# Inverting the delta-rule triangles by diagonal blocks of 32

## The chip, the cores and the metric

The kernel runs on one core of one Trainium2 chip. The metric is the device time of one execution in microseconds (us); the time of a kernel is the median of its runs. The five engines are TensorE (PE), VectorE (DVE), ScalarE (ACT), GpSimd (POOL) and SyncE (SP), and each works through its own queue of instructions in order, held back by semaphores.

## The reference, cut to what matters

A two-layer network on 256 tokens of width 1024 runs: a first block (feed-forward, a mixer, cross attention to a memory, feed-forward) twice, then a second block twice. The mixer has a part with eight heads of 64 that keeps a state and updates it token by token:

```
def step(state, inp):
    r_t, w_t, k_t, v_t, kk_t, a_t = inp
    sa = jnp.einsum('bhij,bhj->bhi', state, -kk_t)
    state = (state * w_t[:, :, None, :] + sa[..., None] * (kk_t * a_t)[:, :, None, :]
             + v_t[..., None] * k_t[:, :, None, :])
    return state, jnp.einsum('bhij,bhj->bhi', state, r_t)
```

The kernel does not run this loop. It cuts the 256 tokens into four chunks of 64. Within a chunk the tokens' corrections depend on each other through a strictly triangular 64 by 64 matrix N per head, and solving for them needs the inverse of I − N. There are 8 heads and 4 chunks, so 32 such inverses in each of the two layers. Everything is float32.

## The kernel before, in words

The 256 tokens lie on 128 partitions in two tiles, t = 0 and 1. A tile holds two chunks: c = 0 on partitions 0 to 63 and c = 1 on 64 to 127. The eight heads are split in two groups g of four (even and odd heads). So there are four groups (t, g), the list `GROUPS4`, each with 4 heads x 2 chunks = 8 triangles, and one PSUM bank for each (4 + 2t + g).

The masked triangles N lie in `MK` (slot 0 of its third dimension), written by DVE at L1137. `T2` holds for each group two running matrices of 4 x 64 columns: the inverse transposed (slot 0) and the inverse (slot 1). `XG` holds an intermediate product.

The inverse is built by doubling. `pe_rw_inv0` (L1161) computes the untransposed triangle; `dve_rw_inv0` masks both down to pairs of tokens and adds the identity (L1170, L1172, L1176). Then five levels, 1 to 5, each join two inverted blocks of size b = 2, 4, 8, 16, 32 to one of 2b: PE computes N times the inverse into PSUM (L1185), DVE masks it to the blocks below the diagonal (L1205), PE multiplies that with the inverse from the other side, once for the inverse transposed (L1194) and, except in level 5, once for the inverse (L1197), and DVE adds the result to both (L1210). Each product is one 64*64 matmul for each head and chunk, the two chunks one after the other on two diagonal quarters of the PE array. Within a level all four groups do their first products, then all four their second ones.

The order of the work is written out by hand, one list for each engine: `pe_mix`, `act_mix`, `dve_mix`. Between the levels stand other steps: on PE transposes for the memory's keys (`pe_kv_turn`, L1660), transposes to token order (L1098), units of the weight stream (L343 to L345), the bonus (L1331) and gate products (L1343, L1344); on DVE the low parts of those transposes (L459), two scalings (L1085, L1088) and the split of weights into a high and a low part (L325), for which ACT makes the high part (L316) and SP loads the raw weights into a ring of four. After level 5 the chunks are solved in turn: `pe_rw_rhs` (L1236), `pe_rw_u` (L1270, which reads `T2`), `pe_rw_state`. `pe_rw_rhs` waits for the last additions of level 5.

Of the kernel before, what the change touches and what calls it, by code (L numbers as in the profile page):

```python
# [9 lines left out]
ACT = mybir.ActivationFunctionType  # L10
ALU = mybir.AluOpType
AX = mybir.AxisListType.X

P = 128
S = 256
NT = S // P
# [6 lines left out]
HD = 64  # L23
# [30 lines left out]
def constants():  # L54

    s = np.arange(P)[:, None]
    t = np.arange(P)[None, :]
    same = (s // 64) == (t // 64)
    c = {}
    c["ident"] = (s == t)  # L60
    decay = -float(np.exp(-0.5))
    c["cums"] = np.concatenate([decay * ((s <= t) & same), decay * ((s < t) & same)], 1)
    c["ones64"] = np.concatenate([(s // 64 == 0), (s // 64 == 1)], 1)
    c["cum"] = np.concatenate([(s + P * k) <= np.arange(S)[None, :] for k in range(NT)], 1)

    i, j = s % 64, np.arange(64)[None, :]
    c["ident64"] = i == j
    c["mask4"] = np.concatenate([i < j, i <= j, i < j, i <= j], 1)
    for lv in range(6):
        b = 1 << lv  # L70
        c[f"low{lv}"] = ((i // (2 * b)) == (j // (2 * b))) & ((i // b) % 2 == 1) & ((j // b) % 2 == 0)
    c["lowT0"] = ((i // 2) == (j // 2)) & (i % 2 == 0) & (j % 2 == 1)
# [57 lines left out]
class Program:  # L130
# [60 lines left out]
    def places1(self):  # L191
# [3 lines left out]
        xn = self.XN.rearrange("p a b -> p (a b)")  # L195
# [9 lines left out]
        self.ZR = self.E2  # L205
        self.MK = self.mem(NT, 8, 4, HD)
        t2 = self.mem(2048)
        self.T2 = [[t2[:, 512 * (2 * t + g):512 * (2 * t + g + 1)].rearrange("p (a h c) -> p a h c", a=2, h=4)
                    for g in range(2)] for t in range(NT)]
        self.XG = [[xn[:, 1024 + 256 * (2 * t + g):1280 + 256 * (2 * t + g)].rearrange("p (h c) -> p h c", h=4)  # L210
                    for g in range(2)] for t in range(NT)]

        flat = lambda x: x.rearrange("p h k -> p (h k)")
# [926 lines left out]

    GROUPS4 = ((0, 0), (0, 1), (1, 0), (1, 1))

    def x4(self, t, g):
        return self.bank(4 + 2 * t + g, 4 * HD).rearrange("p (h c) -> p h c", h=4)

    def t4(self, t, g):
        return self.bank(4 + 2 * t + g)[:, 4 * HD:8 * HD].rearrange("p (h c) -> p h c", h=4)

    def b4(self, n):
        return self.c(n).unsqueeze(1).to_broadcast([P, 4, HD])

    def pe_rw_inv0(self, l):
        pe = self.nc.tensor
        for t, g in self.GROUPS4:
            pe.wait_ge(*self.rw_dve("masked", l, 1, 2 * t + g))
            for i in range(4):
                for c in range(2):
                    cols = slice(t * P + c * HD, t * P + (c + 1) * HD)  # L1160
                    ins = pe.matmul(self.x4(t, g)[c * HD:(c + 1) * HD, i, :], self.AR[HD * g:HD * (g + 1), 0, i, cols],  # L1161
                                    self.BK[HD * g:HD * (g + 1), 0, i, cols], start=True, stop=True, skip_group_check=True)
            self.rw_pe.mark(ins, "inv0", l, t, g)

    def dve_rw_inv0(self, l, groups):
        dve, m = self.nc.vector, self.rw_dve
        for t, g in groups:
            T = self.T2[t][g]
            dve.wait_ge(*m("masked", l, t, 2 + g))
# [5 lines left out]
            dve.wait_ge(*m("TI 0", l, t, g))  # L1175
            m.mark(dve.tensor_tensor(T, T, eye, ALU.add), "T", l, t, g, 0)  # L1176

    def pe_rw_level(self, l, lv):
        pe, m = self.nc.tensor, self.rw_pe
        for t, g in self.GROUPS4:  # L1180
            pe.wait_ge(*self.rw_dve("T", l, t, g, lv - 1))
            for i in range(4):
                for c in range(2):
                    co = slice(c * HD, (c + 1) * HD)
                    ins = pe.matmul(self.x4(t, g)[co, i, :], self.MK[co, t, 2 * i + g, 0, :], self.T2[t][g][co, 1, i, :],  # L1185
                                    start=True, stop=True, skip_group_check=True)
            m.mark(ins, "level x", l, t, g, lv)
        for t, g in self.GROUPS4:
            T, X = self.T2[t][g], self.XG[t][g]
            pe.wait_ge(*self.rw_dve("X", l, t, g, lv))  # L1190
            for i in range(4):
                for c in range(2):
                    co = slice(c * HD, (c + 1) * HD)
                    ins = pe.matmul(self.x4(t, g)[co, i, :], X[co, i, :], T[co, 0, i, :], start=True, stop=True,  # L1194
                                    skip_group_check=True)
                    if lv < 5:
                        ins = pe.matmul(self.t4(t, g)[co, i, :], T[co, 0, i, :], X[co, i, :], start=True, stop=True,  # L1197
                                        skip_group_check=True)
            m.mark(ins, "level", l, t, g, lv)

    def dve_rw_level(self, l, lv):
        dve, m = self.nc.vector, self.rw_dve
        for t, g in self.GROUPS4:
            dve.wait_ge(*self.rw_pe("level x", l, t, g, lv))
            m.mark(dve.tensor_tensor(self.XG[t][g], self.x4(t, g), self.b4(f"low{lv}"), ALU.mult), "X", l, t, g, lv)  # L1205
        for t, g in self.GROUPS4:
            n = 2 if lv < 5 else 1
            T = self.T2[t][g][:, 0:n].rearrange("p a h c -> p (a h c)")
            dve.wait_ge(*self.rw_pe("level", l, t, g, lv))
            m.mark(dve.tensor_tensor(T, T, self.bank(4 + 2 * t + g, 256 * n), ALU.add), "T", l, t, g, lv)  # L1210

# [10 lines left out]
    def pe_rw_rhs(self, l, t, c):  # L1222
# [1 line left out]
        co, cols = slice(c * HD, (c + 1) * HD), slice(t * P + c * HD, t * P + (c + 1) * HD)  # L1224
        first = t == 0 and c == 0
        if c == 0:
            for g in range(2):
                pe.wait_ge(*self.rw_dve("T", l, 1, g, 5))
            pe.wait_ge(*self.rw_act("by token", "v", l, 1))
            if t:  # L1230
                pe.wait_ge(*self.rw_act("u", l, 0, 1))
                pe.wait_ge(*self.rw_dve("gn centred", l, 0))
            for h in range(8):
                hc = slice(h * HD, (h + 1) * HD)
                for both in (slice(0, HD), slice(HD, P)):
                    ins = pe.matmul(self.bank(4)[both, hc], self.MK[both, t, h, 2, :], self.VAL[both, t, hc],  # L1236
                                    start=h == 0, stop=False, skip_group_check=True)
# [761 lines left out]
    def pe_mix(self, l):  # L1999
        pe = self.nc.tensor  # L2000
# [71 lines left out]
        self.pe_rw_level(l, 5)  # L2072
        pe.wait_ge(*self.rw_act("bonus", l))
        self.pe_rw_gate(l, 1, 0)
        self.pe_kv(l, 0, 2)
# [35 lines left out]
    def act_mix(self, l):  # L2111
# [94 lines left out]
    def dve_mix(self, l):  # L2206
# [82 lines left out]
        self.dve_rstd(("mem", l), slot=1)  # L2289
        self.dve_rw_level(l, 4)  # L2290
        self.dve_split(2)
        self.dve_rw_level(l, 5)
        self.dve_split(2)
        self.dve_rw_chunk(l, 0, 0)
        self.dve_split(1)
# [1116 lines left out]
```

## Time and profile before

| | us |
|---|---|
| median of three runs | 1879.29 |
| lowest and highest | 1876.02, 1880.2 |
| the profiled execution's own time | 1879.87 |
| its span | 1878.6 |
| PE busy | 1840.2 (98%) |
| DVE busy | 1172.0 (62%) |
| ACT busy | 928.5 (49%) |

The durations in the rows further down all come from the one profiled execution. The inversion of layer 0 lies between 323 and 376 us of its span, that of layer 1 between 977 and 1032. A float32 matmul leaves two records on PE and two weight loads. A row such as `64*64 64x64 f32` reads: 64 rows and 64 columns of weights, and 64 partitions by 64 moving columns. The duration of one record is its way through the array; records that follow each other overlap.

### The profile page before, as it was taken

To read this page: it belongs to the slowest core of one execution; us is meant where nothing else is said; L and a number is where in the kernel's file an instruction comes from. 1 tells how busy PE (TensorE), PEld (TensorE's weight loads), DVE (VectorE), ACT (ScalarE), POOL (GpSimd) and SP (SyncE) were. 2 spreads that over 40 slices of the span, in tenths; PEclk is the share of its full clock that TensorE was granted. 3 is DMA by queue.
4 is the path that set the end of the run, shared out by engine and by line. 5 is a ranking of instruction groups with operands and counts; after the bars stand their busy time and mean duration, and the time that the engine had idled before them with its cause. 6 is when DMAs were issued, how large, how long until landed. Compare 5 with 4: busy or idle time off the path is not lost.

```text
span 1878.6 us, 27992 instructions
## 1 busy us (share of the span) xinstructions
PE 1840.2 (98%) x11596; PEld 1546.9 (82%) x11596; DVE 1172.0 (62%) x1653; ACT 928.5 (49%) x1413; POOL 93.6 (5%) x59
## 2 busy tenths in 40 slices
PE   7999999999999999999999999999999999999999
PEld 6888788878888888887888888888888888888887
DVE  5555577766655565555777666555688548697556
ACT  5444664234544454446642345444555654556553
POOL 0000010040000000000100400000010000000000
PEclk9999998999999999999999999999999999999999
DMA  6755442023455557554420235655554456554454
GB/s 239 249 189 179 168 146 68 25 80 113 158 190 189 191 173 249 191 189 159 156 68 25 80 112 170 207 189 190 167 167 158 156 193 203 168 171 159 159 186 140
DMA packets 83615, 299.18 MB, mean 159 GB/s; under 512 B 9632, under 2 KB 10784, under 8 KB 83232
## 3 DMA queue, kind: packets, MB, share of 16 engines
q1 hardware_dynamic: 79328, 287.87, 46.4%
q10 hardware_dynamic: 3840, 8.03, 1.2%
q8 instruction: 92, 1.51, 0.3%
q0 software_dynamic: 320, 1.48, 0.2%
q14 instruction: 35, 0.29, 0.0%
HBM read 296.30 MB, written 1.05 MB: 158 GB/s over the span
## 4 chain that ended last, share of the span: by engine, by line
PE 94%; DVE 4%; ACT 1%; issue 1%; DMA 0%; POOL 0%; ACTq 0%; DVEq 0%
PE ps L343 24%; PE ps L345 24%; PE ps L344 24%; PE ps L361 2%; PE ps L362 2%; PE ps L363 2%; PE ps L799 1%; PE ps L1194 1%; PE ps L559 1%; PE ps L1197 1%; DVE wlo L325 1%; PE ps L398 1%; PE ps L1185 1%; PE ps L1597 1%; PE ps L771 1%
## 5 line engine op out<-in xcount | busy, mean ns | idle before, releaser
L325 DVE TENSOR_TENSOR wlo<-raw,whi 128x1024 fp32r<-128x1024 f32 (+1 forms) x546 | 662.7, 1222 | 397.2 <-ACT whi L316 395.9
L316 ACT ACTIVATE whi<-raw 128x1024 fp32r<-128x1024 f32 (+1 forms) x546 | 572.1, 1053 | 487.7 <-PE ps L345 460.6
L343 PE MATMUL ps<-whi,a_hi 128*128 128x512 f32 x1696 | 675.4, 398 | 6.7 <-DVE a_lo L1886 1.7
L345 PE MATMUL ps<-whi,a_lo 128*128 128x512 f32 x1696 | 662.3, 390 | 0.0
L344 PE MATMUL ps<-wlo,a_hi 128*128 128x512 f32 x1696 | 661.3, 390 | 0.0
L343 PEld LDWEIGHTS ps<-whi,a_hi 128*128 128x128 f32 x1696 | 319.1, 188 | 76.3 <-DVE a_lo L1886 2.2
L345 PEld LDWEIGHTS ps<-whi,a_lo 128*128 128x128 f32 x1696 | 318.8, 188 | 68.3
L344 PEld LDWEIGHTS ps<-wlo,a_hi 128*128 128x128 f32 x1696 | 319.4, 188 | 62.2
L343 PE MATMUL ps<-whi,h_hi 128*128 128x512 f32 x320 | 124.9, 390 | 0.0
L345 PE MATMUL ps<-whi,h_lo 128*128 128x512 f32 x320 | 124.6, 389 | 0.0
L344 PE MATMUL ps<-wlo,h_hi 128*128 128x512 f32 x320 | 124.5, 389 | 0.0
L361 PE MATMUL ps<-a_hi,whi 128*128 128x256 f32 (+2 forms) x304 | 88.0, 290 | 2.5 <-issue 2.5
L362 PE MATMUL ps<-a_lo,whi 128*128 128x256 f32 (+2 forms) x304 | 85.9, 283 | 0.0
L363 PE MATMUL ps<-a_hi,wlo 128*128 128x256 f32 (+2 forms) x304 | 85.9, 283 | 0.0
L345 PEld LDWEIGHTS ps<-whi,h_lo 128*128 128x128 f32 x320 | 60.1, 188 | 12.5
L344 PEld LDWEIGHTS ps<-wlo,h_hi 128*128 128x128 f32 x320 | 60.1, 188 | 12.3
L343 PEld LDWEIGHTS ps<-whi,h_hi 128*128 128x128 f32 x320 | 60.1, 188 | 12.3
L581 ACT ACTIVATE arena<-ps,small 128x256 f32<-128x256 f32 x88 | 36.9, 470 | 67.2 <-PE ps L345 67.2
L623 DVE SCALAR_TENSOR_TENSOR arena<-ps,small,arena 128x256 f32<-128x256 f32 x88 | 38.5, 479 | 40.1 <-ACT arena L581 40.1
L361 PEld LDWEIGHTS ps<-a_hi,whi 128*128 128x128 f32 (+2 forms) x304 | 57.0, 187 | 4.2 <-issue 3.8
L491 POOL TENSOR_TENSOR small<-small,minus_half 128x2 f32<-128x2 f32 x10 | 7.0, 700 | 1061.1 <-DVE small L484 703.6
L362 PEld LDWEIGHTS ps<-a_lo,whi 128*128 128x128 f32 (+2 forms) x304 | 57.0, 188 | 0.2
(317 smaller groups left out, 1792.9 us busy)
## 6 DMA issues: line engine op xcount, KB each, us to landing
raw<-stream SPq DMA_DIRECT2D x546, 512.0 KB, 3.4
arena<-rows ACTq DMA_DIRECT2D x2, 1026.0 KB, 13.4
arena<-mem ACTq DMA_DIRECT2D x2, 1024.0 KB, 9.7
arena<-lora ACTq DMA_DIRECT2D x2, 768.0 KB, 6.8
arena<-rows ACTq DMA_DIRECT2D x2, 512.0 KB, 4.4
const_tables<-consts POOLq DMA_DIRECT2D x1, 901.0 KB, 4.8
arena<-band POOLq DMA_DIRECT2D x1, 544.0 KB, 4.1
x_res<-x SPq DMA_DIRECT2D x1, 512.0 KB, 3.7
```

Source lines behind the costliest of these rows:

```text
L316: self.split_hi.mark(act.activation(self.weights(self.whi, u), self.weights(self.raw, u), ACT.Copy), u)
L325: self.split_lo.mark(dve.tensor_tensor(self.weights(self.wlo, u), self.weights(self.raw, u), self.weights(self.whi, u).bitcast(F32), ALU.s ...
L343: pe.matmul(out, a_h, hi, start=start, stop=False, skip_group_check=True)
L344: pe.matmul(out, a_h, lo, start=False, stop=False, skip_group_check=True)
L345: last = pe.matmul(out, a_l, hi, start=False, stop=True, skip_group_check=True)
L361: pe.matmul(out, hi, self.AHI[:, kt, :], start=first and kt == 0, stop=False, skip_group_check=True)
L362: pe.matmul(out, hi, self.ALO[:, kt, :], start=False, stop=False, skip_group_check=True)
L363: last = pe.matmul(out, lo, self.AHI[:, kt, :], start=False, stop=True, skip_group_check=True)
L398: ins = pe.transpose(self.bank(banks[k % 4])[:, t * P:(t + 1) * P], self.X[:, t, k * P:(k + 1) * P], self.c("ident"))
L559: ins = pe.transpose(self.bank(banks[kk])[:, t * P:(t + 1) * P], self.h_buffer(j)[:, t, kk * P:(kk + 1) * P], self.c("ident"))
L581: self.silu.mark(act.activation(self.SG[:, t, :], self.bank((2 if j == 1 else 4) + t, 256), ACT.Silu, scale=self.rs(0, t)), key, j, t)
L623: self.h_ready.mark(dve.scalar_tensor_tensor(self.h_buffer(j)[:, t, :], self.bank((2 if j == 1 else 4) + t)[:, 256:512], self.rs(0, t), se ...
```

## The change

The blocks of a triangle are now kept in two sizes. Each 64 by 64 triangle is taken as two diagonal blocks of 32 and the block between them. The levels 1 to 4 work only on the diagonal blocks of 32. The 128 partitions then hold four such blocks, and each product is one 32*32 matmul for each head and block; the four blocks lie on the four diagonal sixteenths of the PE array (`TRIANGLES`). The running matrices are 4 x 32 columns wide in place of 4 x 64 (`TC`), as are the mask and the intermediate product. `pe_rw_inv0` computes both orientations for the blocks, and DVE masks both in one operation. The last level (`pe_rw_last`) computes the block between the two diagonal blocks by two products of 32*32 matmuls, a pair for each head. ACT copies the inverted diagonal blocks into the full 64-wide matrices `TI` with a zero below (`act_rw_last`), and ACT and DVE copy the remaining block there (`act_rw_last_out`, `dve_rw_last`). `pe_rw_rhs` waits for these copies, and `pe_rw_u` reads `TI`. The constant tables change with the masks: 512 columns go and 225 come.

```diff
     def pe_rw_inv0(self, l):
...
             for i in range(4):
-                for c in range(2):
-                    cols = slice(t * P + c * HD, t * P + (c + 1) * HD)
-                    ins = pe.matmul(self.x4(t, g)[c * HD:(c + 1) * HD, i, :], self.AR[HD * g:HD * (g + 1), 0, i, cols],
-                                    self.BK[HD * g:HD * (g + 1), 0, i, cols], start=True, stop=True, skip_group_check=True)
+                for b in range(4):
+                    rows, cols = slice(32 * b, 32 * b + 32), slice(t * P + 32 * b, t * P + 32 * b + 32)
+                    pe.matmul(self.x4(t, g)[rows, i, :], B[:, i, cols], A[:, i, cols], start=True, stop=True,
+                              skip_group_check=True)
+                for b in range(4):
+                    rows, cols = slice(32 * b, 32 * b + 32), slice(t * P + 32 * b, t * P + 32 * b + 32)
+                    ins = pe.matmul(self.t4(t, g)[rows, i, :], A[:, i, cols], B[:, i, cols], start=True, stop=True,
+                                    skip_group_check=True)
...
     def dve_rw_inv0(self, l, groups):
...
-            m.mark(dve.tensor_tensor(T[:, 0], self.MK[:, t, g::2, 0, :], self.b4("lowT0"), ALU.mult), "TIT 0", l, t, g)
             dve.wait_ge(*self.rw_pe("inv0", l, t, g))
-            m.mark(dve.tensor_tensor(T[:, 1], self.x4(t, g), self.b4("low0"), ALU.mult), "TI 0", l, t, g)
-            eye = self.c("ident64").unsqueeze(1).to_broadcast([P, 8, HD])
+            ps = self.bank(4 + 2 * t + g, 256).rearrange("p (a h c) -> p a h c", a=2, h=4)
+            m.mark(dve.tensor_tensor(T, ps, pairs, ALU.mult), "pairs", l, t, g)
...
     def pe_rw_level(self, l, lv):
...
             for i in range(4):
-                for c in range(2):
-                    co = slice(c * HD, (c + 1) * HD)
-                    ins = pe.matmul(self.x4(t, g)[co, i, :], self.MK[co, t, 2 * i + g, 0, :], self.T2[t][g][co, 1, i, :],
+                for rows, cols in self.TRIANGLES:
+                    ins = pe.matmul(self.x4(t, g)[rows, i, :], self.MK[rows, t, 2 * i + g, 0, cols], T[rows, 1, i, :],
                                     start=True, stop=True, skip_group_check=True)
...
             for i in range(4):
-                for c in range(2):
-                    co = slice(c * HD, (c + 1) * HD)
-                    ins = pe.matmul(self.x4(t, g)[co, i, :], X[co, i, :], T[co, 0, i, :], start=True, stop=True,
+                for rows, cols in self.TRIANGLES:
+                    pe.matmul(self.x4(t, g)[rows, i, :], X[rows, i, :], T[rows, 0, i, :], start=True, stop=True,
+                              skip_group_check=True)
+                for rows, cols in self.TRIANGLES:
+                    ins = pe.matmul(self.t4(t, g)[rows, i, :], T[rows, 0, i, :], X[rows, i, :], start=True, stop=True,
                                     skip_group_check=True)
-                    if lv < 5:
-                        ins = pe.matmul(self.t4(t, g)[co, i, :], T[co, 0, i, :], X[co, i, :], start=True, stop=True,
-                                        skip_group_check=True)
...
+    def pe_rw_last(self, l):
...
+            for i in range(4):
+                for up, down in self.HALVES:
+                    ins = pe.matmul(self.x4(t, g)[down, i, :], self.MK[up, t, 2 * i + g, 0, 32:HD],
+                                    self.TC[t][up, g, 1, i, :], start=True, stop=True, skip_group_check=True)
...
+            for i in range(4):
+                for up, down in self.HALVES:
+                    ins = pe.matmul(self.last4(t)[up, g, i, :], self.XG[t][g][down, i, :], self.TC[t][down, g, 0, i, :],
+                                    start=True, stop=True, skip_group_check=True)
...
+    def act_rw_last(self, l):
...
+        for t in range(NT):
+            act.wait_ge(*self.rw_dve("T", l, t, 1, 4))
+            m.mark(act.activation(self.TI[t][:, :, :, 0:32], self.TC[t][:, :, 0], ACT.Copy, scale=self.c("upper")),
+                   "left", l, t)
+            m.mark(act.activation(self.TI[t][:, :, :, 32:HD], self.TC[t][:, :, 0], ACT.Copy), "right", l, t)
...
+    def dve_rw_last(self, l):
+        dve, m = self.nc.vector, self.rw_dve
+        for t, g in self.GROUPS4:
+            dve.wait_ge(*self.rw_pe("level x", l, t, g, 5))
+            m.mark(dve.tensor_copy(self.XG[t][g], self.x4(t, g)), "X", l, t, g, 5)
+        for t in range(NT):
+            dve.wait_ge(*self.rw_pe("level", l, t, 1, 5))
+            dve.wait_ge(*self.rw_act("right", l, t))
+            m.mark(dve.tensor_copy(*self.last_out(t, 0)), "triangle", l, t)
...
     def pe_rw_rhs(self, l, t, c):
...
-            for g in range(2):
-                pe.wait_ge(*self.rw_dve("T", l, 1, g, 5))
+            pe.wait_ge(*self.rw_dve("triangle", l, 1))
+            pe.wait_ge(*self.rw_act("triangle", l, 1))
...
     def pe_rw_u(self, l, t, c):
...
-            ins = pe.matmul(self.bank(5)[co, hc], self.T2[t][h % 2][co, 0, h // 2, :], self.RHS[co, hc], start=True,
+            ins = pe.matmul(self.bank(5)[co, hc], self.TI[t][co, h % 2, h // 2, :], self.RHS[co, hc], start=True,
...
     def act_mix(self, l):
...
         self.act_split(2)
+        self.act_rw_last(l)
         self.act_rw_bonus_out(l, 0)
         self.act_rw_gate(l, 0, 1)
+        self.act_rw_last_out(l)
         self.act_rw_gate(l, 1, 0)
```

In `pe_mix` and `dve_mix` the calls of level 5 become `pe_rw_last(l)` and `dve_rw_last(l)`, at the same places.

## Rows read from the trace of the kernel before

**Rows 1.** The page, parts 1 and 4: busy time by engine, and the chain.
```profile
PE 1840.2 (98%) x11596; PEld 1546.9 (82%) x11596; DVE 1172.0 (62%) x1653; ACT 928.5 (49%) x1413; POOL 93.6 (5%) x59
...
PE 94%; DVE 4%; ACT 1%; issue 1%; DMA 0%; POOL 0%; ACTq 0%; DVEq 0%
```
**Rows 2.** PE's groups by line and form: names, shapes, count, busy us, mean ns, idle.
```profile
L1194 PE MATMUL ps<-arena 64*64 64x64 f32 x640 | 35.0, 219 | 1.7 <-DVE arena L1205 1.7
L1197 PE MATMUL ps<-arena 64*64 64x64 f32 x512 | 30.6, 218 | 0.0
...
L1185 PE MATMUL ps<-arena 64*64 64x64 f32 x640 | 22.4, 227 | 1.0 <-DVE arena L1176 1.0
...
L1161 PE MATMUL ps<-arena 64*64 64x64 f32 x128 | 5.4, 259 | 3.5 <-DVE arena L1137 3.5
```
**Rows 3.** The chain, 320 to 385 us: start us, us, what.
```profile
327.89 1.71 PE ps L1098 x8
...
331.99 0.33 DVE arena L1170
...
332.69 0.69 DVE arena L1176
...
334.77 0.79 DVE a_lo L459 x2
...
335.94 0.34 PE ps L1194 x4
...
339.82 0.13 PE ps L1197 x4
...
340.58 1.22 DVE arena L1085
341.80 0.79 DVE a_lo L459 x2
...
342.97 0.34 PE ps L1194 x4
...
347.55 0.87 PE ps L1098 x8
...
367.91 1.68 PE ps L1331 x16
...
371.61 2.01 PE ps L1185 x64
373.62 1.87 PE ps L1194 x64
375.49 1.06 PE ps L1343 x2
...
377.59 0.43 PE ps L343
```
**Rows 4.** PE's timeline, merged: start us, us to the last end, names, shapes, count.
```profile
314.31 0.81 PE L1125 MATMUL ps<-arena 64*64 64x128 f32 x17
...
381.92 1.10 PE L1258 MATMUL ps<-arena 64*64 64x64 f32 x31
...
387.34 1.09 PE L1285 MATMUL ps<-arena 64*64 64x64 f32 x16
...
391.31 1.09 PE L1241 MATMUL ps<-arena 128*64 128x128 f32 x8
```
**Rows 5.** DVE's timeline, 317 to 392 us, and ACT's copies by form.
```profile
335.48 1.41 DVE L1205 TENSOR_TENSOR arena<-ps,const_tables 128x256 f32<-128x256 f32 x4
...
339.98 0.69 DVE L1210 TENSOR_TENSOR arena<-arena,ps 128x512 f32<-128x512 f32 x1 [0.25 <-PE ps L1197]
...
L448 ACT ACTIVATE a_hi<-ps,arena 128x256 fp32r<-128x256 f32 x16 | 6.7, 470 | 37.8 <-PE ps L1660 37.8
```
**Rows 6.** Busy time by stretch: PE, PEld, DVE, ACT, POOL, granted clock, DMA share, GB/s.
```profile
326.20:329.60 3.40, 3.40 (x18) 3.40 (x18) 2.34 (x6) 1.19 (x2) 0.00 (x0) 0.52 0.00 0
...
336.00:340.00 4.00, 4.00 (x129) 3.93 (x130) 2.96 (x7) 0.00 (x0) 0.00 (x0) 1.00 0.00 0
```

More of the change, by code:

```diff
@@ L66, in constants @@
     i, j = s % 64, np.arange(64)[None, :]
-    c["ident64"] = i == j
     c["mask4"] = np.concatenate([i < j, i <= j, i < j, i <= j], 1)
-    for lv in range(6):
+    i, j = s % 32, np.arange(32)[None, :]
+    c["eye32"] = i == j
+    c["pairs"] = np.concatenate([(i // 2 == j // 2) & (i < j), (i // 2 == j // 2) & (i > j)], 1)
+    for lv in range(1, 5):
         b = 1 << lv
         c[f"low{lv}"] = ((i // (2 * b)) == (j // (2 * b))) & ((i // b) % 2 == 1) & ((j // b) % 2 == 0)
-    c["lowT0"] = ((i // 2) == (j // 2)) & (i % 2 == 0) & (j % 2 == 1)
+    c["upper"] = (s // 32) % 2 == 0
     c["causal"] = np.where(t <= s, 0.0, NEG)
@@ L207, in places1 @@
         t2 = self.mem(2048)
-        self.T2 = [[t2[:, 512 * (2 * t + g):512 * (2 * t + g + 1)].rearrange("p (a h c) -> p a h c", a=2, h=4)
-                    for g in range(2)] for t in range(NT)]
-        self.XG = [[xn[:, 1024 + 256 * (2 * t + g):1280 + 256 * (2 * t + g)].rearrange("p (h c) -> p h c", h=4)
+        self.TC = [t2[:, 512 * t:512 * (t + 1)].rearrange("p (g a h c) -> p g a h c", g=2, a=2, h=4) for t in range(NT)]
+        self.TI = [t2[:, 1024 + 512 * t:1536 + 512 * t].rearrange("p (g h c) -> p g h c", g=2, h=4) for t in range(NT)]
+        self.XG = [[xn[:, 1024 + 128 * (2 * t + g):1152 + 128 * (2 * t + g)].rearrange("p (h c) -> p h c", h=4)
                     for g in range(2)] for t in range(NT)]
@@ L1143, with last4 @@
     GROUPS4 = ((0, 0), (0, 1), (1, 0), (1, 1))
+    TRIANGLES = tuple((slice(32 * b, 32 * b + 32), slice(32 * (b % 2), 32 * (b % 2) + 32)) for b in range(4))
+    HALVES = tuple((slice(HD * c, HD * c + 32), slice(HD * c + 32, HD * c + HD)) for c in range(2))
     def x4(self, t, g):
-        return self.bank(4 + 2 * t + g, 4 * HD).rearrange("p (h c) -> p h c", h=4)
+        return self.bank(4 + 2 * t + g, 128).rearrange("p (h c) -> p h c", h=4)
     def t4(self, t, g):
-        return self.bank(4 + 2 * t + g)[:, 4 * HD:8 * HD].rearrange("p (h c) -> p h c", h=4)
-    def b4(self, n):
-        return self.c(n).unsqueeze(1).to_broadcast([P, 4, HD])
+        return self.bank(4 + 2 * t + g)[:, 128:256].rearrange("p (h c) -> p h c", h=4)
+    def last4(self, t):
+        return self.bank(4 + 2 * t, 256).rearrange("p (g h c) -> p g h c", g=2, h=4)
     def pe_rw_inv0(self, l):
@@ L1157, in pe_rw_inv0 @@
             pe.wait_ge(*self.rw_dve("masked", l, 1, 2 * t + g))
+            A, B = (x[HD * g:HD * (g + 1), 0] for x in (self.AR, self.BK))
             for i in range(4):
-                for c in range(2):
-                    cols = slice(t * P + c * HD, t * P + (c + 1) * HD)
-                    ins = pe.matmul(self.x4(t, g)[c * HD:(c + 1) * HD, i, :], self.AR[HD * g:HD * (g + 1), 0, i, cols],
-                                    self.BK[HD * g:HD * (g + 1), 0, i, cols], start=True, stop=True, skip_group_check=True)
+                for b in range(4):
[6 more added lines that the diff above has]
+                                    skip_group_check=True)
             self.rw_pe.mark(ins, "inv0", l, t, g)
@@ L1180, in pe_rw_level @@
         for t, g in self.GROUPS4:
+            T = self.TC[t][:, g]
             pe.wait_ge(*self.rw_dve("T", l, t, g, lv - 1))
             for i in range(4):
-                for c in range(2):
-                    co = slice(c * HD, (c + 1) * HD)
-                    ins = pe.matmul(self.x4(t, g)[co, i, :], self.MK[co, t, 2 * i + g, 0, :], self.T2[t][g][co, 1, i, :],
+                for rows, cols in self.TRIANGLES:
+                    ins = pe.matmul(self.x4(t, g)[rows, i, :], self.MK[rows, t, 2 * i + g, 0, cols], T[rows, 1, i, :],
                                     start=True, stop=True, skip_group_check=True)
@@ L1202, in dve_rw_level @@
         dve, m = self.nc.vector, self.rw_dve
+        low = self.c(f"low{lv}").unsqueeze(1).to_broadcast([P, 4, 32])
         for t, g in self.GROUPS4:
             dve.wait_ge(*self.rw_pe("level x", l, t, g, lv))
-            m.mark(dve.tensor_tensor(self.XG[t][g], self.x4(t, g), self.b4(f"low{lv}"), ALU.mult), "X", l, t, g, lv)
+            m.mark(dve.tensor_tensor(self.XG[t][g], self.x4(t, g), low, ALU.mult), "X", l, t, g, lv)
         for t, g in self.GROUPS4:
-            n = 2 if lv < 5 else 1
@@ L1208, in dve_rw_level @@
-            T = self.T2[t][g][:, 0:n].rearrange("p a h c -> p (a h c)")
+            T = self.TC[t][:, g].rearrange("p a h c -> p (a h c)")
             dve.wait_ge(*self.rw_pe("level", l, t, g, lv))
-            m.mark(dve.tensor_tensor(T, T, self.bank(4 + 2 * t + g, 256 * n), ALU.add), "T", l, t, g, lv)
+            m.mark(dve.tensor_tensor(T, T, self.bank(4 + 2 * t + g, 256), ALU.add), "T", l, t, g, lv)
+    def pe_rw_last(self, l):
+        pe, m = self.nc.tensor, self.rw_pe
+        for t, g in self.GROUPS4:
+            pe.wait_ge(*self.rw_dve("T", l, t, g, 4))
+            for i in range(4):
+                for up, down in self.HALVES:
+                    ins = pe.matmul(self.x4(t, g)[down, i, :], self.MK[up, t, 2 * i + g, 0, 32:HD],
+                                    self.TC[t][up, g, 1, i, :], start=True, stop=True, skip_group_check=True)
+            m.mark(ins, "level x", l, t, g, 5)
+        for t, g in self.GROUPS4:
+            pe.wait_ge(*self.rw_dve("X", l, t, g, 5))
+            for i in range(4):
+                for up, down in self.HALVES:
+                    ins = pe.matmul(self.last4(t)[up, g, i, :], self.XG[t][g][down, i, :], self.TC[t][down, g, 0, i, :],
+                                    start=True, stop=True, skip_group_check=True)
+            m.mark(ins, "level", l, t, g, 5)
@@ new lines, in act_rw_last, with last_out @@
+    def act_rw_last(self, l):
+        act, m = self.nc.scalar, self.rw_act
+        for t in range(NT):
[3 more added lines that the diff above has]
+            m.mark(act.activation(self.TI[t][:, :, :, 32:HD], self.TC[t][:, :, 0], ACT.Copy), "right", l, t)
+    def last_out(self, t, c):
+        up = self.HALVES[c][0]
+        return self.TI[t][up, :, :, 32:HD], self.last4(t)[up]
@@ new lines, in act_rw_last_out @@
+    def act_rw_last_out(self, l):
+        act, m = self.nc.scalar, self.rw_act
+        for t in range(NT):
+            act.wait_ge(*self.rw_pe("level", l, t, 1, 5))
+            act.wait_ge(*m("right", l, t))
+            m.mark(act.activation(*self.last_out(t, 1), ACT.Copy), "triangle", l, t)
+    def dve_rw_last(self, l):
+        dve, m = self.nc.vector, self.rw_dve
+        for t, g in self.GROUPS4:
+            dve.wait_ge(*self.rw_pe("level x", l, t, g, 5))
+            m.mark(dve.tensor_copy(self.XG[t][g], self.x4(t, g)), "X", l, t, g, 5)
+        for t in range(NT):
+            dve.wait_ge(*self.rw_pe("level", l, t, 1, 5))
+            dve.wait_ge(*self.rw_act("right", l, t))
+            m.mark(dve.tensor_copy(*self.last_out(t, 0)), "triangle", l, t)
@@ L2071, in pe_mix @@
         self.pe_rw_gate(l, 0, 1)
-        self.pe_rw_level(l, 5)
+        self.pe_rw_last(l)
         pe.wait_ge(*self.rw_act("bonus", l))
@@ L2291, in dve_mix @@
         self.dve_split(2)
-        self.dve_rw_level(l, 5)
+        self.dve_rw_last(l)
         self.dve_split(2)
```

9 lines of the change are left out of this document (5 added, 4 removed).

## The prediction

> **What bounds the kernel now.** I read the page first: the engine totals say that TensorE (PE) is busy 98% of the span, and the chain that ended last runs 94% on PE and 4% on VectorE (DVE) [rows 1]. So what counts is PE time, and the waits in which PE stands. Next the groups by line and form: the triangle inversion is the four lines L1161, L1185, L1194 and L1197, all 64*64 matmuls with 64 columns [rows 2]. For both layers they are 128 + 640 + 640 + 512 = 1920 records, 960 a layer (a float32 matmul leaves two records). "Mean ns of one" is the latency, not the price, since neighbours overlap. So I went to the chain in order of time through layer 0's inversion, 323 to 376 us [rows 3]. The reader is to see two kinds of stretch there: full runs of PE records, such as 64 in 1.87 us (29.2 ns each), and stretches in which the chain leaves PE for DVE (331.99 to 335.94, and 339.95 to 342.97). In those PE is waiting, and DVE's short element-wise operations are the price. Layer 1 repeats the pattern.
>
> **How matmuls overlap.** Everything hangs on the pitch of one record once tiles are 32 by 32. The timeline [rows 4] gives it for other tilings; I take (duration − latency of the last) / (records − 1). L1285 keeps to one 64*64 tile of the array: (1.09 − 0.22)/15 = 58 ns. L1258 alternates between two diagonal tiles: (1.10 − 0.22)/30 = 29 ns, exactly half. So the two tiles run as independent streams. L1125 uses all four 64*64 tiles, with 128 columns: (0.81 − 0.27)/16 = 34 ns, against (1.09 − 0.28)/7 = 116 ns for L1241, which streams 128 columns through one tile. That is 3.4 streams. So four streams do exist. The period of one stream follows the weight columns: 105 ns with 128 (L1331, 1.68/16, two moving columns) [rows 3], 58 ns with 64; the same step downwards makes 32 to 35 ns with 32, an estimate. Four streams then give 8 to 9 ns a record.
>
> **The change, part by part (a layer).**
> *Record counts.* First products: 64 become 4 groups x 4 heads x 8 matmuls x 2 = 256. Each of levels 1 to 4: 64 + 128 become 128 + 256. The last level stays at 64 + 64, but on two streams of 32*32. Sum 960 → 1920: twice the records, so twice the weight loads and twice what PE's sequencer must hand out.
>
> *The pitch.* No row shows a 32*32 tile. From below: 8.3 ns (four free streams). From above: 29.2 ns, what it is now [rows 3], if something other than the tile's own period set it. The densest row of the trace is 29 ns a record, so nothing here shows how fast PE can be fed. I take 11 ns: 8.3 x 4/3.4 = 9.8 by what L1125 reaches of its four streams, and a little for the start of each group. L1125 is the row most like the new code, the only one with four tiles at work.
>
> The Trainium skill ("TensorE: Matmul & The Clock Gate", section "Wait — 56ns, not 53.3ns?") says that start-to-start of matmuls never drops below about 25 ns however few the columns; no row here lies below it, so the trace neither supports nor refutes it; it would make rival C true, and by C's line 25 ns come to +16 us a layer, 1911. Its page "TensorEngine Tiling (Array Packing)", section "Instruction Overhead", warns for the same reason not to take a tiling factor from a dimension that is already small.
>
> *First products and their masks.* PE's 2.7 us for L1161 (5.4 for both layers) are paced by DVE's masking, for which PE stood 3.5 us over both layers [rows 2]. At 11 ns they are 2.8 us: at nothing. On DVE each group had 0.33 + 0.34 + 0.69 = 1.36 us (the second like the first, L1172) [rows 3] and gets two operations of 256 elements, 0.68. Two of the four groups lie on the chain (331.99 to 334.77), so −1.4 us. The other two lie beside waits for PE.
>
> *Level 1.* L1194/L1197 take 335.94 to 339.95, 128 records in 3.74 us without the start; now 256 x 11 ns = 2.8: −0.9. The first half (L1185) is already covered by DVE.
>
> *Level 2.* Same −0.9. In the wait from 339.95 to 342.97 DVE does its last addition (339.98 to 340.58, 0.60; 0.34 for 256 elements in place of 512), L1085 (1.22 with its end) and L459 (0.79), both unchanged, and a mask of 128 instead of 256 elements (L1205, (1.41 − 0.41)/3 = 0.33; no row for 128, so between 0 and 0.33; I take 0.2, since 0.33 and 0.60 make 0.06 + 0.27 per 256 elements) [rows 3, 5]. Saved 0.4. L1185's 128 x 11 = 1.4 us stays under these 2.4. Together −1.3. Once this is done DVE's unchanged L1085 and L459 are what is late: a faster PE gains nothing more there.
>
> *Level 3.* By the same counts −0.9, and −0.3 at its front: PE leads there now, and once it is faster DVE's queue (L459, and L1088, as long as L1085) is last, itself 0.4 shorter. −1.2. *Level 4* is all PE: the 2.01 us of L1185 (as in the last level, 371.61) become 1.4, and −0.9: −1.5.
>
> *Last level.* 2.01 + 1.87 us for 128 records [rows 3] on two streams: half of 32 to 35, so 16 to 17 ns, 1.05 us each: −1.8. The solve gets a new wait, for the corner copies of DVE and ACT, and everything behind it on PE would stand. But a gate (375.49 to 377.59, 2.1 us) and then a whole weight unit lie between the last product and the solve [rows 3], so the copies are at nothing; without that cover 0.4 us each, twice on each engine. On DVE two weight splits are queued behind its corner copies, which wait for ACT's; PE needs these splits a unit later, and the ring holds four.
>
> *ScalarE (ACT).* Four new copies of 128x256 at 0.47 us and less [rows 5], and two of 32 partitions, 2.7 us in all, behind its two weight splits. They wait for DVE's level 4 additions, long done then; queued behind them are the bonus copy and the gate copy. The bonus product ends at 369.6 (367.91 + 1.68) and PE asks for its copy at 375.49 [rows 3]: covered. Bounds 0 and 2.7 us a layer, I take 0. The constants are smaller; their load is covered too. No DMA is moved.
>
> **Sum.** 1.4 + 0.9 + 1.3 + 1.2 + 1.5 + 1.8 = 8.1 us a layer, 16 for two. (DVE and PE parts never cover each other in this sum: each stretch is counted where the chain runs.) The profiled execution took 1879.87 us (span 1878.6), 0.6 above the median 1879.29, so 1879.9 − 16 = 1863.6, and as a median 1863.
>
> **Rivals.**
> A. *Four free streams*, 8.3 ns. Levels gain 1.6 instead of 0.9 in the second half (256 x 8.3 = 2.1), level 4 another 0.35, level 3 little: 11 us a layer, 1857. For it: L1258's exact half. Against it: L1125's 3.4 of 4. Chance 0.27.
> B. *The feed binds at half of today's pitch*, 14.6 ns. Levels gain nothing on PE; DVE's 1.4 + 0.4 + 0.3 and the last level's 1.8 stay: 3.9 a layer, 1872. Chance 0.12.
> C. *The other side: a floor per record.* PE hands out loads and matmuls at a fixed pace, and the doubled count is paid. At 29.2 ns the second halves take 7.5 us instead of 3.74 (+15 for four), the first halves +5.5 behind DVE's cover, the first products 7.5 instead of 2.7 (+3.4 with DVE's gain off): +24 a layer, 1928. It decides from about 17 ns, where the line between 14.6 ns (−3.9) and 29.2 ns (+24) crosses zero; the floor can lie anywhere between. For it: every dense row sits at 29 ns. Against it: one tile at 58 and two at 29 is what free streams give, a coincidence if it were a floor. Chance 0.20.
> D. *The clock.* The granted clock fell to the lower level (1.2 GHz) at 326.2 to 329.6, behind a stretch in which PE stood and did narrow work [rows 6]. There eight transposes (L1098) take 1.71 us instead of 0.87 [rows 3]. Narrower tiles on a PE that waits more could bring five such falls a layer, 1.7 us each: all of the gain, 1880. Against it: 336 to 340 kept 1.00 on 64*64 tiles [rows 6]. Chance 0.07.
>
> **How the numbers follow.** Forecast 0.34, A 0.27, B 0.12, C 0.20, D 0.07. The forecast's own range is 1859 to 1868. A change below 0.2% (3.8 us) can't be told from none here. Faster: forecast, A and B, a little of D less the tail of each: 0.70. Same: D's middle and the near end of C, 0.08. Slower: 0.22. The range for 8 in 10 holds A with one more microsecond below, D, and the near part of C: 1854 to 1905; left out are the far half of C, beyond a floor of 23 ns (0.10), and some 0.07 below.
>
> **What would show it.** The pitch: runs of the level lines in the chain, 256 records in 2.8 us (2.1 by A, 3.7 by B, over 6.4 by C). DVE: masks of 128 elements and additions of 256, and the stretch from level 1's last addition to level 2's first product 0.4 us shorter. The last level 1.05 us a half. PE must not stand before the solve; if it waits for ACT there, the cover was wrong. The granted clock in the stage decides D. The prediction is wrong if a level record costs over 14 ns.

## The result: slower, 1911.79 us

| | before | after |
|---|---|---|
| median, us | 1879.04 (4 runs) | 1911.79 (4 runs) |
| lowest and highest | 1876.02, 1880.2 | 1904.81, 1920.48 |
| the profiled execution's own time | 1879.87 | 1906.46 |
| its span | 1878.6 | 1905.2 |
| granted TensorE clock, mean over the span | 0.99 | 0.975 |

The ratio is 1.018, with a 95% interval of 1.0148 to 1.0212. The whole interval lies above 1, so the kernel is slower; whether by more than 2% is left open. The change costs 33 us where a gain of 16 was forecast.

The page of the kernel after, parts 1, 3 and 4, answers to [rows 1]: engine totals, the queue that carries the engines' instructions, the chain by engine.

```profile
PE 1831.0 (96%) x13516; PEld 1537.3 (81%) x13516; DVE 1153.0 (61%) x1641; ACT 933.8 (49%) x1425; POOL 93.6 (5%) x59
...
q8 instruction: 107, 1.75, 0.4%
...
PE 92%; DVE 3%; issue 3%; ACT 1%; DMA 0%; POOL 0%; ACTq 0%; DVEq 0%
```

PE has 1920 records more, as counted, and yet is busy 9 us less. "Issue", time in which an engine waits for nothing that the profile shows, went from 1% to 3% of the chain. And q8, the instruction queue, moved 107 packets in place of 92 (1.75 MB in place of 1.51): 15 more of 16 KB each. A record on PE comes with a weight load, so 1920 records more are 3840 instructions more, and 3840 / 15 = 256. The totals say the same: with its own waits for semaphores, PE has 23,559 instructions in the trace of before and 27,399 in that of after, and by 256 these are 92.0 and 107.0, the packets of q8. Instructions come in blocks of 256.

PE's groups by line and form, for the new lines (busy us, mean ns | idle just before them, and what ended it), answer to [rows 2].

```profile
L1205 PE MATMUL ps<-arena 32*32 32x32 f32 x1024 | 27.6, 220 | 19.5 <-issue 19.0 <-DVE arena L1217 0.5
L1208 PE MATMUL ps<-arena 32*32 32x32 f32 x1024 | 27.6, 220 | 11.2 <-issue 11.2
L1197 PE MATMUL ps<-arena 32*32 32x32 f32 x1024 | 13.0, 205 | 4.3 <-issue 4.3
L1173 PE MATMUL ps<-arena 64*32 64x32 f32 x256 | 6.6, 228 | 1.9 <-issue 1.9
L1169 PE MATMUL ps<-arena 64*32 64x32 f32 x256 | 6.6, 231 | 5.2 <-DVE arena L1140 3.5 <-issue 1.8
```

Ahead of these lines, in both layers together, PE stood 19.0 + 11.2 + 4.3 + 1.9 + 1.8 = 38.2 us for nothing visible. In [rows 2] no such idle time is shown: there PE waited only for DVE. The chain of the kernel after in order of time (start us, us, what) shows the pattern; compare [rows 3].

```profile
331.02 0.06 PE ps L1205 x8
...
332.52 1.69 issue
...
334.55 0.11 PE ps L1205 x8
...
336.14 1.80 issue
...
343.32 1.53 issue
...
346.78 1.80 issue
...
349.00 1.04 PE ps L1719 x4
350.05 1.69 PE ps L1101 x8
...
353.94 2.19 issue
...
383.98 1.04 PE ps L1230 x58
385.11 0.92 PE ps L1237 x59
...
388.13 0.43 PE ps L346
```

At first eight records take 0.06 us, 8 ns each: the array does what four free streams would do. Then the clock falls and eight take 0.11 us. And about every 3.5 us PE stands, mostly for 1.5 to 2.4 us. Counted in the trace, with records, loads and PE's own waits for semaphores together, PE stands at its instructions 4289, 4545 and 4801, and later at 5313, 5569, 6081, 6337, 6849 and 7105: always a multiple of 256 apart. Each pause holds the arrival of one 16 KB packet of q8. The trace also shows how far the supply runs ahead. After a pause the next packet starts 1.0 to 1.4 us after PE has entered a block, and in a dense stretch PE enters the next block 3.4 to 3.8 us after that entry. Behind full-width work PE crosses one boundary without standing (5825 at 352.59 us, 6593 at 367.58) and stands at the very next one (356.13 and 371.22). So no more than one block is ready ahead of the one that PE works on. Level 2's second half runs from 341.77 to 349.00: 256 records in 7.2 us, 28 ns a record, where 2.8 us were forecast.

The queues in the same 60 us, 320 to 380, of the kernel before and then of the kernel after (packets, MB, share of 16 engines' time):

```profile
q8 instruction: 9, 0.15, 1.0%
```

```profile
q8 instruction: 14, 0.23, 1.6%
```

Finally the granted clock (the third value from the end; behind it the share of time in which the DMA engines were busy, 0.02, so that little but these packets was moved) in the kernel after; [rows 6] had one fall of 3.4 us in this stage.

```profile
330.70:351.20 20.50, 13.29 (x664) 12.19 (x664) 7.51 (x19) 2.20 (x7) 0.00 (x0) 0.51 0.02 5
351.20:358.00 6.80, 4.06 (x362) 3.52 (x360) 3.43 (x8) 0.93 (x2) 0.52 (x1) 0.97 0.02 5
```

From the last masking before the inversion (L1140 at 315.91, L1137 at 323.04 before) to the unit behind the last level (388.13, and 377.59 before) layer 0 takes 72.2 us in place of 54.6, and layer 1, by the same marks, 74.2 in place of 57.1. That is 17.7 + 17.1, +34.8 us. The profiled spans differ by less, 26.6, mainly because the one of before had a clock fall from 278 to 292 us, ahead of the inversion, that the one of after had not. The stretch of both, before first:

```profile
278.00:292.00 14.00, 14.00 (x58) 9.78 (x57) 4.58 (x9) 0.98 (x4) 2.02 (x1) 0.52 0.01 4
```

```profile
278.00:292.00 14.00, 14.00 (x116) 12.16 (x115) 8.68 (x15) 3.86 (x11) 1.22 (x1) 1.00 0.01 1
```

That is why stages are compared here and not spans.

### The profile page after: what moved, and what is told of

Its sections match the earlier page's. It is cut to its first block, busy times and chain, and to the rows that moved or that the text cites. A ratio compares the mean times of both kernels' runs of the same rounds, so it can differ in the third digit from the quotient of the medians.

```text
span 1905.2 us, 31840 instructions
## 1 busy us (share of the span) xinstructions
PE 1831.0 (96%) x13516; PEld 1537.3 (81%) x13516; DVE 1153.0 (61%) x1641; ACT 933.8 (49%) x1425; POOL 93.6 (5%) x59
## 3 DMA queue, kind: packets, MB, share of 16 engines
q10 hardware_dynamic: 3840, 8.03, 1.2%
q8 instruction: 107, 1.75, 0.4%
HBM read 296.15 MB, written 1.05 MB: 156 GB/s over the span
## 4 chain that ended last, share of the span: by engine, by line
PE 92%; DVE 3%; issue 3%; ACT 1%; DMA 0%; POOL 0%; ACTq 0%; DVEq 0%
PE ps L346 24%; PE ps L348 24%; PE ps L347 24%; PE ps L364 2%; PE ps L366 2%; PE ps L365 2%; PE ps L802 1%; PE ps L562 1%; PE ps L1205 1%; DVE wlo L328 1%; PE ps L1208 1%; PE ps L401 1%; PE ps L774 1%; PE ps L2603 1%; PE ps L1197 1%
```

## The experiments

Two theories stood at the start of the experiments. *Supply*: PE gets its instructions in blocks of 256, some 3.5 us apart at the least, whatever they are; before, 128 records of 29.2 ns (3.74 us) used up a block just as fast as the next came, so doubled counts are paid in full. *Rival*: the narrow tiles themselves, through the clock or through waits between PE and DVE, cost the time. All ratios are to the kernel before, run beside them. The kernel after was not run again, so differences to its 1911.79 us are between separate sets of runs.

**count_doubled** keeps the kernel before and only cuts each 64*64 matmul of the five levels into two of 64*32.

```diff
-                for c in range(2):
-                    co = slice(c * HD, (c + 1) * HD)
-                    ins = pe.matmul(self.x4(t, g)[co, i, :], self.MK[co, t, 2 * i + g, 0, :], self.T2[t][g][co, 1, i, :],
+                for b in range(4):
+                    co, o, m_ = slice(b // 2 * HD, b // 2 * HD + HD), slice(32 * b, 32 * b + 32), slice(b % 2 * 32, b % 2 * 32 + 32)
+                    ins = pe.matmul(self.x4(t, g)[o, i, :], self.MK[co, t, 2 * i + g, 0, m_], self.T2[t][g][co, 1, i, :],
...
```

> The kernel before, in which each 64*64 matmul of levels 1 to 5 is issued as two of 64*32: the same products, the same 64 columns streamed, the same DVE work, but 896 more records a layer (each a load and a matmul). Theory (supply): PE's instructions come in 16 KB blocks of 256, and a block takes at least about 3.5 us; a level then needs 768 instructions, 10.5 us in place of 5.6, partly under waits for DVE, so 15 to 22 us more a layer: 1909 to 1924 us, with gaps put down to issue after every 256 instructions. Rival (narrow 32*32 tiles cost more on the array, or the clock falls because they do little work): nothing changes, 1875 to 1883 us.

Measured: 1909.67 (4 runs, 1905.6 to 1914.38), ratio 1.0161 [1.0141, 1.0181]. The mean clock of its runs was 0.986 to 0.991, against 0.99 in the profile of before. Its chain:

```profile
336.02 0.11 PE ps L1199 x8
...
338.47 1.21 issue
...
345.12 1.74 issue
```

The clock in the stage, from the end of its last fall (330.09 us) to behind the last level:

```profile
330.20:384.00 53.80, 42.25 (x1855) 36.62 (x1855) 31.35 (x59) 10.39 (x20) 1.22 (x2) 1.00 0.08 24
```

Eight records take 0.11 us, 14 ns each, half of 29: the array does the doubled count in the old time. And still 30 us go, in pauses at each block, with the clock up. The count alone gives nearly the whole loss. (It adds 896 records a layer, the change 960; q8 moved 106 packets, 14 more than before, and 2 x 1792 / 256 = 14.)

**records_added** is the kernel after, with the first products of levels 1 to 4 issued twice; **records_removed** is the kernel after without the products of L1208, its masks emptied so that the numbers stay finite (it computes the identity in place of the inverses): 512 records a layer more, and 512 less.

```diff
-            for i in range(4):
+            for i in (0, 1, 2, 3, 0, 1, 2, 3):
...
```

```diff
...
-                for rows, cols in self.TRIANGLES:
-                    ins = pe.matmul(self.t4(t, g)[rows, i, :], T[rows, 0, i, :], X[rows, i, :], start=True, stop=True,
...
```

> The changed kernel with the first products of levels 1 to 4 issued twice: 512 records (1024 instructions, four blocks) more a layer. Supply theory: four blocks of 3.5 us, 14 us a layer, near 1940 us. Rival (the array's own pitch, 8 ns a record in full runs): 512 x 8 ns = 4 us a layer, near 1920 us.

> The changed kernel without the second half of each level's last products (L1208, the inverse that is not transposed) and with masks of zeros, so that the inverse is the identity: 512 records (four blocks) fewer a layer, all else in place. Supply theory: 14 us less a layer, near 1884 us, lower if the clock also stays up. Rival (array pitch): 4 us a layer, near 1903 us.

Measured: added 1947.68 (1942.22 to 1950.38), ratio 1.0359 [1.0335, 1.0382]; removed 1882.88 (10 runs, 1871.6 to 1893.24), ratio 1.001 [0.9988, 1.0032]. Over both layers each moves 1024 records, 8 blocks: +36 and -29 us around 1911.8, so 4.5 and 3.6 us a block; their queues moved 115 and 99 packets, 8 more and 8 fewer than 107. The removal came out as expected, the addition 8 us above the expected 1940. The time follows the count down to about the time of before.

**burst_32x32**, **burst_32x8**, **burst_64x32** measure the cost by itself: 1024 more matmuls in one place, with nothing to wait for.

```diff
+            if (l, lv, t, g) == (0, 1, 1, 1):
+                for r in range(64):
+                    for i in range(4):
+                        for rows, cols in self.TRIANGLES:
+                            pe.matmul(self.x4(t, g)[rows, i, 0:32], X[rows, i, :], T[rows, 0, i, 0:32], start=True,
...
```

(32x8 has `0:8`; 64x32 stands in the kernel before, 128 rounds on the two 64*64 tiles, with 32 columns.)

> The kernel after with 1024 more 32*32 matmuls of 32 columns, once (layer 0, level 1, before the last group's second products), into a place that the real products then overwrite: 2048 records, 4096 PE instructions, 16 blocks of 256, and no wait among them. It measures the disputed cost by itself. Supply theory (3.5 us a block whatever the array does): +56 us, 1962 to 1972, with PE standing every 256 instructions while nothing holds it. Array alone at 8 ns a record: +17 us, 1925 to 1930. A floor of 25 ns between starts: +51 us, but with starts spread evenly and no pauses.

> The same burst with 8 moving columns in place of 32. Supply theory: the same +56 us as burst_32x32, within 2 us. If the array set the price: clearly less than burst_32x32.

> The kernel before with 1024 more 64*64 matmuls of 32 moving columns at the same place, on its two diagonal tiles: 2048 records, 4096 instructions. The level's own records of 64 columns take 29.2 ns each, so the array would need at most 60 us and, if a record's period follows the columns, some 30 us. Supply theory: 56 us again, 1933 to 1940. Array theory: 1909 to 1915, or 1940 if the period follows the weights alone.

Measured (2 runs each): 1972.28, 1976.29 and 1943.19, which is +60.5, +64.5 (over 1911.79) and +63.6 us (over 1879.58) for 16 blocks, 3.8 to 4.0 us a block. By supply 56 us were expected of each. With two runs of each, 5 to 9 us apart in the first two, the 4 us between 32x32 and 32x8 can't be told from noise. The chain of burst_32x32, and its instruction queue from 345 to 385 us:

```profile
350.24 1.80 issue
352.04 1.93 PE ps L1207 x128
353.97 1.53 issue
```

```profile
q8 instruction: 11, 0.18, 1.8%
```

128 records, pause, 128 records: one block each, 11 in 40 us, 3.64 us apart. PE waits for no other engine. In burst_32x8 the same 128 records take 1.89 us instead of 1.93, at the same granted clock of 0.50:

```profile
349.27 1.89 PE ps L1207 x128
351.16 1.57 issue
```

so the columns do not matter, as expected by supply. burst_64x32 shows one long run, and near its end a short pause:

```profile
338.50 56.72 PE ps L1196 x1941
395.22 0.09 issue
395.31 3.22 PE ps L1196 x105
```

29.2 ns a record, with 32 columns as with the 64 of [rows 3]. The array's pace and that of the supply lie close here (3.73 and about 3.65 us a block), but the entries into the blocks tell them apart. From 338.95 to 387.48 us PE enters 13 blocks in a row 3.73 us apart, without a change, where those of burst_32x32 vary between 3.45 and 4.00: there the array sets the pace. Then two blocks begin late, 3.82 and 4.00 us behind the ones before, with the gap at the boundary: there it was the supply. So the period of a 64*64 tile did not fall with the moving columns.

**last_by_blocks** does the one part of the change that does not raise the count: the kernel before, its last level by 32*32 blocks, with DVE's copies alone.

```diff
...
-        self.pe_rw_level(l, 5)
+        self.pe_rw_last(l)
...
```

> The kernel before with the last level alone taken from the change: the block below the diagonal by 32*32 matmuls on two streams, written by four DVE copies straight into the 64-wide matrices, no ACT copies; the record count stays 960 a layer. If a block of instructions is waiting when the level starts (PE does slow, wide work ahead of it), the 128 records run at 16 to 17 ns instead of 29: 1.8 us less a layer, 1875.5 us. If the supply binds there too (28 ns a record), no change: 1879 us. Slower than before would mean that the new waits for DVE's copies are exposed.

Measured: 1879.78 (12 runs, 1873.18 to 1880.68), ratio 0.9998 [0.9989, 1.0007]: no change. The chain of its profiled execution suggests why.

```profile
364.73 1.22 PE ps L1380 x2
365.95 1.69 PE ps L1229 x58
367.80 1.53 PE ps L1236 x58
369.32 2.00 PE ps L1379 x2
371.33 2.00 PE ps L1380 x2
...
374.06 0.43 PE ps L345
```

The clock fell (at 365.49 us) behind the bonus products (16 records of two columns). The halves are only a little shorter than in [rows 3], and the gate, 1.06 + 1.05 there, takes 2.00 + 2.00; the weight unit behind it runs at half speed too (0.43 a product for 0.23). A theory of its own followed: put full-width work between the bonus and the last level.

**blocks_bonus_first** moves the bonus ahead of the weight unit, **blocks_gate_between** also puts a gate product between the halves of the last level, and **before_bonus_first** is their control (no blocks, only the order, which is the edit shown):

```diff
-        self.pe_kv(l, 0, 1)
         pe.wait_ge(*self.rw_act("by token", "k", l, 1))
         self.pe_rw_bonus(l, 0)
+        self.pe_kv(l, 0, 1)
         self.pe_rw_gate(l, 0, 1)
```

> The kernel before with only the last level by blocks of 32 (as last_by_blocks), and on PE the bonus products moved ahead of the weight unit kv(0,1), so that a full-width unit stands between them and the last level. Theory (the gain of last_by_blocks was given back by a clock fall behind bonus, gate and a narrow last level): the granted clock stays at 1.00 from 365 to 380 us, the halves stay at 1.5 to 1.7 us or less, and the time is 1.5 to 4 us under last_by_blocks, 1876 to 1878.5. Rival (the clock falls whenever the last level is narrow, or the supply of instructions takes the gain anyway): 1879 to 1881.

> As blocks_bonus_first, and the first gate product (full width) stands between the two halves of the last level. It covers DVE's copies between the halves and splits the burst of narrow matmuls. If instructions arrive in blocks with one block in reserve, the second half finds its instructions ready: 0.5 to 1.5 us a layer under blocks_bonus_first, 1874 to 1878. Rival (bursts of 128 matmuls are short enough anyway): the same as blocks_bonus_first within 1 us.

> The kernel before with only the bonus products moved ahead of kv(0,1); nothing else. It is the control for the two others: 1878.5 to 1880.5 by the theory that the order matters only with the narrow last level; if the order itself is worth something, 1876 to 1878.

Measured (12 runs each): 1875.76, ratio 0.9984 [0.9971, 0.9996]; 1875.57, 0.9984 [0.9973, 0.9995]; 1876.55, 0.9981 [0.9966, 0.9996]. All three lie 3 to 4 us below the kernel before, and so below last_by_blocks too. The stretch from 360 to 380 us, of last_by_blocks and of blocks_bonus_first, and then the last level in blocks_bonus_first and in the control:

```profile
360.00:380.00 20.00, 20.00 (x213) 13.24 (x213) 6.29 (x12) 3.49 (x5) 0.00 (x0) 0.66 0.24 79
```

```profile
360.00:380.00 20.00, 20.00 (x390) 15.53 (x387) 10.69 (x18) 3.97 (x6) 0.00 (x0) 1.00 0.24 81
```

```profile
370.84 1.04 PE ps L1229 x58
371.97 0.92 PE ps L1236 x59
```

```profile
370.84 2.01 PE ps L1185 x64
372.85 1.87 PE ps L1194 x64
```

The clock stays up, and the level costs 1.9 us less a layer. Yet the medians of the two differ by 0.8 us where 3.8 should show. The control contradicts what was expected of it: the order alone is worth 3 us (by its interval 1 to 6). In layer 1 of the kernel before the same fall came behind the bonus, with full-width gates and 64*64 tiles:

```profile
1025.53 1.46 PE ps L1344 x2
1026.99 3.15 PE ps L1185 x64
```

So the fall is not the narrow last level's alone. Why the blocks' 3.8 us do not show in the median stays open; the control's runs fall into three groups, about 1871.5, 1876.5 and 1882.8 us with mean clocks of 0.995, 0.992 and 0.988, so the groups lie further apart (5 to 6 us) than the effect is large.

**after_spread** is the kernel after with full-width work between the bursts, the instructions the same: kv(0,0) between level 4's halves, the bonus ahead of kv(0,1), a gate product between the last level's halves.

> The kernel after with full-width work put between the bursts: kv(0,0) between the halves of level 4, the bonus ahead of kv(0,1), a gate product between the halves of the last level. Same instructions, same count. Supply theory with about one block of 256 instructions in reserve: in the kernel after the supply rests from 361 to 368 us while kv(0,1), bonus and gate run, and PE starves before and behind that; spread out, 1.5 to 4 us a layer come back, 1904 to 1909 against 1912. If the reserve were several blocks deep the order could not matter: 1911 to 1913.

Measured: 1908.5 (5 runs, 1902.45 to 1919.09), ratio 1.0144 [1.0121, 1.0166], against 1.018 [1.0148, 1.0212]. The 3 us lie in the direction of a short reserve, but the intervals overlap: not settled by this run's times. What its expectation says of 361 to 368 us is misread: the transposes and the unit kv(0,0) ran there, and kv(0,1), bonus and gate from 375.90 to 383.98. That the reserve is short is shown instead by the entries into the blocks, read above.

## Why the prediction was wrong

**The step that failed is "The pitch"**: "nothing here shows how fast PE can be fed. I take 11 ns." The array's part of it was even too careful: 8 ns a record at full clock. The price of a record in the levels was 28 ns (level 2's second half), because 256 instructions, 128 records, take about 3.6 us to arrive. All that was built on 11 ns fell with it: the four -0.9 us of the second halves did not come, and in the levels and the first products PE stood for 38.2 us over both layers.

**Rival C was what happened**, with its price nearly met: over 6.4 us for 256 records was its mark, 7.2 was measured. Its time, 1928, was too high by 16. It left out what stayed good in the forecast (the last level's 1.8, DVE's shorter operations), and full-width work between the bursts lets the supply catch up: the unit at 377 us and the bonus stood before the last level, and that level ran without a pause. Its mechanism was drawn too loosely: not a pace of each record but of blocks, with something in reserve. The rule of the Trainium skill ("TensorE: Matmul & The Clock Gate", section "Wait — 56ns, not 53.3ns?") that starts never come closer than 25 ns is not what acts: starts lay 8 ns apart. That 25 ns gave 1911, and 1912 was measured, is a coincidence. What bears on it stands in the Trainium skill under "Runtime: NRT & Kernel Launch", section "Instruction fetch mechanics": an engine's instructions are refilled in blocks of 16 KB. The blocks agree with the trace. For how much is held the section has two figures, 128 KB for PE, which would be eight blocks, and "only 2 cache lines" of 16 KB. The traces fit the second, one block in work and one ahead: with eight held and full, PE would not stand at the second boundary behind full-width work, as it does at 356.13 and 371.22 us. The same section says that crossing a block is mostly hidden because dispatch is slower than the refill; bursts of small matmuls refute that here, by 1.5 to 2.4 us a block.

**The trace of before had the hint.** That "every dense row sits at 29 ns" was taken as array periods of 58 halved. It was that, and it was also nearly all that the supply could carry: 128 records of 29.2 ns use up a block in 3.73 us, and a block takes about 3.65. The page's q8 row (92 packets, 1.51 MB) would have given 256 instructions a packet. The smallest distance between two packets in the inversion of before, 3.8 us, showed that nothing there had asked for more; that the bound lay just below it, only denser runs could show.

**First products and masks**: forecast -1.4 us a layer. DVE's two operations of a group take 0.44 us to the second one's start and 0.35 to the next group's (327.90), 0.79 a group in place of 1.36 (0.68 forecast). The saving is there on DVE, but PE stood before L1169 and L1173 for 3.7 us over both layers.

```profile
327.11 0.41 DVE L1185 TENSOR_TENSOR arena<-ps,const_tables 128x256 f32<-128x256 f32 x1
327.55 0.43 DVE L1188 TENSOR_TENSOR arena<-arena,const_tables 128x256 f32<-128x256 f32 x1
...
329.48 0.68 DVE L1217 TENSOR_TENSOR arena<-ps,const_tables 128x128 f32<-128x128 f32 x3
331.09 0.29 DVE L1217 TENSOR_TENSOR arena<-ps,const_tables 128x128 f32<-128x128 f32 x1 [0.94 <-PE ps L1197]
```

**Masks of 128 elements**: 0.2 us taken; L1217 has (0.68 - 0.29)/2, 0.2. Right, and worth nothing where PE stood for its instructions, since DVE was no longer what came last.

**Last level**: 1.05 us a half forecast, 1.04 and 0.92 measured. Right in the mechanism and in the size.

**ScalarE's copies at nothing**: right. The four of 128x256 ran from 381.3 to 382.8, the bonus copy behind them was done at 382.9, and PE asked for it at 386.03.

```profile
381.28 0.49 ACT L1246 ACTIVATE arena<-arena,const_tables 128x256 f32<-128x256 f32 x1
...
382.69 0.16 ACT L1397 ACTIVATE small<-ps 128x16 f32<-128x16 f32 x1
...
385.57 0.88 ACT L1259 ACTIVATE arena<-ps 32x256 f32<-32x256 f32 x2 [0.95 <-PE ps L1237]
```

**The clock (rival D)** came as well, behind the pauses: four falls in layer 0, 41 us in all, at 317 to 324, 331 to 351, 358 to 365 and 372 to 379, and four in layer 1, 48 us in all. What it costs is bounded by the full-width work in them. Against the durations at full clock, two sets of transposes L1101 lose 0.84 us each, three of L1719 (1.04 for 0.59) 0.45 each, and some twelve products of weight units 0.2 each: 5 to 6 us of the 17.7, and less, since the supply went on meanwhile. The dense records themselves lose little by it: in the bursts a block of them takes 1.93 us at the lower clock, well inside the 3.4 to 4.0 us until the next block is there. The split between the two is not settled further; that the supply alone suffices is shown by count_doubled, which lost 30 us with the clock at 1.00 in the levels.

## What to carry to other kernels

Count PE's instructions as a resource of their own: here a stretch of matmuls gets at most about 256 instructions (128 float32 records) each 3.5 to 4 us, and whatever makes tiles smaller and more numerous gains nothing below some 29 ns a record unless full-width work lies between. Look at the instruction queue in the profile of before, at its packets and their distance in the densest stretch, ahead of any sum that shrinks matmuls. And look at what stands behind thin work on PE: moving sixteen products of two columns ahead of a weight unit was worth 3 us here, more than the blocks; that a clock fall less is the reason is likely from the traces, but not shown run by run.

## What the runs showed of the hardware

- A PE block is 256 instructions of 64 bytes (16,384 bytes a packet). In burst_32x32 the distance from one packet's start to the next was its transfer (0.88 to 1.44 us) and 2.3 to 2.7 us on top: 3.3 to 4.0 us. In the inversion of the kernel before a packet mostly starts within some 40 instructions of a block's boundary, and PE never stands for one. No more than one block was ready ahead in any dense stretch of the kernel after.
- Four 32*32 tiles take a record each 8 ns at 2.4 GHz (0.06 us for eight) and 14 ns at 1.2 GHz (0.11 us for eight; 1.93 us for 128 with the first one's 0.2).
- With 8 moving columns instead of 32 a record was hardly shorter (1.89 and 1.93 us for 128, both at 1.2 GHz), and on 64*64 tiles 32 columns cost what 64 do, 29.2 ns.
- Executions of one kernel differ with the mean granted clock: groups 5 to 6 us apart, at 0.995, 0.992 and 0.988, in the control's twelve runs.
